# State-space decays by bfloat16 selector matmuls, in two decay and two score banks

## The reference, cut to what matters

```
a_cum = jnp.cumsum(dtc * A.reshape(SSM_GROUPS, SSM_HPG), axis=2)
diff = a_cum[:, :, :, None] - a_cum[:, :, None]
decay = jnp.exp(jnp.where(tril, diff, -jnp.inf))
cb = jnp.einsum('bclgn,bcsgn->bclsg', Cc, Bc)
y_diag = jnp.einsum('bclsgj,bcsgjp->bclgjp', cb[..., None] * decay, xdt)
```

## Time and profile before

| | |
|---|---|
| median of three runs | 2743.5 us |
| span of the profiled execution, first to last instruction | 2729.7 us |
| the median less that span (launch and end; the profile shows no more of its execution) | 13.8 us |
| conv, group a / group b | until about 114 us / 681 to 815 us |
| ssd, group a / group b | 114 to 170 us / 815 to 905 us |
| busy over the span: TensorE / VectorE / ScalarE / GpSimd | 74% / 53% / 25% / 54% |
| mean granted TensorE clock | 0.870 |

### The profile page before, as it was taken

How to read it: one execution, slowest core, us unless ns; L and a number is a source line. 1 busy time by engine, 2 the same in 40 slices (tenths; PEclk the granted TensorE clock), 3 DMA queues, 4 the chain that set the end, 5 groups by cost and what they waited for, 6 DMA issues and landing times. The chain is left out here.

```text
span 2729.7 us, 31629 instructions
## 1 busy us (share of the span) xinstructions
PE 2018.4 (74%) x10995; PEld 1286.9 (47%) x10995; DVE 1456.9 (53%) x3506; ACT 673.6 (25%) x2035; POOL 1478.6 (54%) x1493
## 2 busy tenths in 40 slices
PE   8999989987977979989988946755267776655044
PEld 6888875655655656654444722322144443111010
DVE  3331013226897975457731568778686665106910
ACT  4441016313547320015531112321011110001000
POOL 1120000006556766656654777787867777567775
PEclk9899989988988999989989967886588987868577
DMA  5414344344895899889889979999999999999998
GB/s 181 169 62 140 129 179 186 134 164 168 302 345 190 323 391 400 326 339 331 333 328 398 347 250 374 411 394 341 398 343 412 409 411 402 402 401 402 409 409 326
DMA packets 209780, 843.32 MB, mean 309 GB/s; under 512 B 25752, under 2 KB 32728, under 8 KB 190104
## 3 DMA queue, kind: packets, MB, share of 16 engines
q0 software_dynamic: 170912, 644.95, 61.8%
q1 hardware_dynamic: 38712, 196.36, 19.3%
HBM read 821.80 MB, written 23.54 MB: 310 GB/s over the span
## 5 line engine op out<-in xcount | busy, mean ns | idle before, releaser
L3604 POOL DMA_INDIRECT e_ring<-in_peer_u,e_idx x523 | 615.2, 1176 | 300.1 <-DVE e_dot L3768 142.7
L3768 DVE CUSTOM_DVE_ANT_0 e_ring<-e_ring,e_h 128x1024 f32<-128x1024 f32 x523 | 631.5, 1243 | 68.7 <-PEq L1159 22.0
L3604 POOL DMA_INDIRECT e_ring<-in_peer_v,e_idxT x487 | 510.7, 1049 | 258.5 <-issue 132.4
L3671 PE MATMUL ps<-e_ring,e_wz 128*32 128x512 f32 x1948 | 316.8, 698 | 261.9 <-DMA e_ring<-in_peer_v,e_idxT 152.9
L3671 PEld LDWEIGHTS ps<-e_ring,e_wz 128*32 128x32 f32 x1948 | 66.9, 119 | 416.7 <-issue 405.5
L363 PE MATMUL ps<-hT_ahead,wb 128*128 128x320 f32 x384 | 110.6, 443 | 0.9 <-DMA wb<-in_weights 0.9
L363 PEld LDWEIGHTS ps<-hT_ahead,wb 128*128 128x128 f32 x384 | 72.9, 195 | 30.1 <-issue 2.7
L1815 POOL CAST ra_atf<-ra_at 128x32 f32<-128x32 uint32 x8 | 1.7, 211 | 149.7 <-DVE ra_hit L1808 149.7
L3812 DVE TENSOR_TENSOR e_x<-e_x,ps 128x512 f32<-128x512 f32 x10 | 6.4, 684 | 141.8 <-PE ps L3671 141.8
L1183 POOL MEMSET inda<- 128x256 f32 x1 | 0.3, 311 | 147.7 <-POOLq L4071 147.7
L3671 PE MATMUL ps<-ring_pair,e_wz 128*32 128x512 f32 x152 | 63.2, 730 | 17.2 <-DMA e_ring<-in_peer_v,e_idxT 11.3
(11 more groups left out here) (778 smaller groups left out, 4610.4 us busy)
## 6 DMA issues: line engine op xcount, KB each, us to landing
wb<-in_weights SPq DMA_DIRECT2D x65, 1024.0 KB, 7.3
e_ring<-in_weights SPq DMA_DIRECT2D x36, 1024.0 KB, 4.9
wb<-in_late_weights SPq DMA_DIRECT2D x6, 2048.0 KB, 10.9
room<-in_late_weights SPq DMA_DIRECT2D x6, 2048.0 KB, 15.7
h<-in_weights SPq DMA_DIRECT2D x10, 1024.0 KB, 8.3
xs<-in_weights SPq DMA_DIRECT2D x9, 1024.0 KB, 7.9
e_ring<-in_peer_u,e_idx POOLq DMA_INDIRECT x523, 8.7
e_ring<-in_peer_v,e_idxT POOLq DMA_INDIRECT x487, 10.6
```

The lines of the kernel that those rows point to most:

```text
L3604: nc.gpsimd.indirect_dma_start(out=self.room(place), out_offset=None, in_=k.peer_u if kind == "u" else k.peer_v, in_offset=off).then_inc(s ...
L3671: last = nc.tensor.matmul(k.ps[32 * b:32 * b + 32, self.SUMS + i, :], self.wz[:, at:at + 32], self.room(self.v_at[n])[:, 512 * i:512 * i + ...
L3768: v.tensor_tensor_reduce(uu, uu, self.h[:, tile % 2, :], 1.0, 0.0, ALU.mult, ALU.add, self.dot[:, tile % 2, t:t + 1]).then_inc(self.dotted, 1)
```

## The change

The running sums, with heads on the partitions, are made once per chunk in conv, in PSUM bank 4, three times over (partitions 0 to 31, 32 to 63, 64 to 95). VectorE splits each into three bfloat16 pieces whose sum is the float32 value, one on each block of 32 partitions. A matmul with a matrix of ones and zeros as one operand (`head_rows`, 96x32) then picks a head and adds the three pieces. The row term a_cum[l] becomes four such matmuls, with the pieces as the moving operand and a broadcast column of the selector as the weight; the column term -a_cum[s] becomes one matmul with the pieces as the weight and the negative selector, broadcast to 4x128, moving. Nothing is left for the bias, and one activation covers four heads. Decays and scores have two banks each, and the orders of TensorE and VectorE change.

```diff
+            for rows_of, fill in ((k.head_rows, 1.0), (k.head_rows_neg, -1.0)):
+                own(gp.memset(rows_of[:], 0.0))
+                for piece in range(PIECES_F32):
+                    own(gp.affine_select(out=rows_of[:], in_=rows_of[:], compare_op=ALU.not_equal, fill=fill,
+                                         base=-HEADS * piece, pattern=[[-1, HEADS]], channel_multiplier=1))
...
+                for i, t in enumerate(g.prompt):
+                    for lo in range(0, SPLIT, HEADS):
+                        last = nc.tensor.matmul(k.ps[lo:lo + HEADS, 4, P * i:P * i + P], k.da[:, t, :], k.cum[:], start=True,
+                                                stop=True)
...
+            def split_sums():
+                sums = k.ps[0:SPLIT, 4, 0:NP]
+                parts = [slice(HEADS * i, HEADS * i + HEADS) for i in range(PIECES_F32)]
+                own(v.tensor_copy(k.cum_pieces[:], sums))
+                own(v.tensor_tensor(k.cum_rest[:], sums, k.cum_pieces[:], ALU.subtract))
+                own(v.tensor_copy(k.cum_middle[:], k.cum_rest[:]))
+                own(v.tensor_tensor(k.cum_rest[:], k.cum_rest[:], k.cum_middle[:], ALU.subtract))
+                v.tensor_copy(k.cum_pieces[parts[1]], k.cum_middle[parts[1]])
+                v.tensor_copy(k.cum_pieces[parts[2]], k.cum_rest[parts[2]]).then_inc(split, 1)
...
+                if f == 9:
+                    split_sums()
...
+        DECAY, SCORE = [1, ex.TURN], [0, ex.SUMS]
...
-                if q:
-                    pe.wait_ge(exped, q)
-                bank = k.ps[:, 1, :].rearrange("p (h l) -> p h l", h=4)
+                if q >= 2:
+                    pe.wait_ge(exped, q - 1)
+                bank = k.ps[:, DECAY[q % 2], :].rearrange("p (h l) -> p h l", h=4)
+                sums = k.cum_pieces[:, P * c:P * c + P]
+                h0 = gr * PER + 4 * i
                 mm(bank, k.identb[:], k.later[:].rearrange("p (a l) -> p a l", a=1).broadcast_to([P, 4, P]),
                    start=True, stop=False, skip_group_check=True)
+                mm(bank, sums, k.head_rows_neg[:, h0:h0 + 4].rearrange("p (h a) -> p h a", a=1).broadcast_to([SPLIT, 4, P]),
+                   start=False, stop=False, skip_group_check=True)
                 for j in range(4):
-                    hh = gr * PER + 4 * i + j
-                    last = mm(bank[:, j, :], k.da[:, t0 + c, hh:hh + 1].broadcast_to([P, P]), k.cum[:],
+                    last = mm(bank[:, j, :], k.head_rows[:, h0 + j:h0 + j + 1].broadcast_to([SPLIT, P]), sums,
                               start=False, stop=(j == 3), skip_group_check=True)
...
-                if u:
-                    pe.wait_ge(weighted, 2 * u)
+                if u >= 2:
+                    pe.wait_ge(weighted, 2 * u - 2)
...
             for u in range(U + 1):
                 if u < U:
                     decays(u, 0)
+                    decays(u, 1)
...
-                if u:
-                    within(u - 1)
                 if u < U:
                     score(u)
                     ex.pe(2 * u)
-                    decays(u, 1)
                 if u:
+                    within(u - 1)
                     from_state(u - 1)
                     to_state(u - 1)
...
-                for j in range(4):
-                    hh = gr * PER + 4 * i + j
-                    last = a.activation(MT[:, q % 4, j, :], k.ps[:, 1, j * P:j * P + P], ACT.Exp,
-                                        bias=k.nacum[:, t0 + c, hh:hh + 1])
-                last.then_inc(exped, 1)
+                a.activation(MT[:, q % 4], k.ps[:, DECAY[q % 2], :].rearrange("p (h l) -> p h l", h=4),
+                             ACT.Exp).then_inc(exped, 1)
...
                 if u < U:
                     weigh(u, 0)
-                if u:
-                    finish(u - 1)
-                if u < U:
                     ex.dve(2 * u)
                     weigh(u, 1)
                 if u:
+                    finish(u - 1)
                     carry(u - 1)
```

More of the change, by code:

```diff
@@ L50 @@
 PKEYS = 128
+PIECES_F32 = 3
+SPLIT = PIECES_F32 * HEADS
 EPS = 1e-6
@@ L314, in stage_conv @@
                                    for i in range(5))
-        stepped, steps_copied, raw, raw_copied, abs_done, exp_done, plus_one, ln_done, step_done, summed, negated = (
+        (stepped, steps_copied, raw, raw_copied, abs_done, exp_done, plus_one, ln_done, step_done, summed, negated,
+         split) = (
             sem(n) for n in ("stepped", "steps_copied", "raw", "raw_copied", "abs", "exp", "plus_one", "ln", "step",
-                             "summed", "negated"))
+                             "summed", "negated", "split"))
         steps_by_head = k.Bs[0:HEADS, 0:N]
@@ L334, in stage_conv @@
         k.conv_done = dict(tailed=(tailed, F), activated=(activated, F), gathered=(gathered, B_TILES),
-                           written=(written, 32) if g.sample else None)
+                           split=(split, 1), written=(written, 32) if g.sample else None)
         @block.sync
@@ L626, in by_channel, with scores_of @@
             return t.rearrange("p (h q) -> p h q", q=HP)
+        DECAY, SCORE = [1, ex.TURN], [0, ex.SUMS]
+        assert g.first or ex.done + ex.tokens <= min(ex.u_at[P - 1], ex.v_at[0])
+        def scores_of(u):
+            return k.ps[:, SCORE[u % 2], 0:P]
         @block.gpsimd
@@ L687, in score @@
                 tok = slice(P * c, P * c + P)
-                if u:
-                    pe.wait_ge(weighted, 2 * u)
-                mm(k.ps[:, 0, 0:P], k.BT[:, gr, tok], k.CT[:, gr, tok], start=True, stop=True).then_inc(scored, 1)
+                if u >= 2:
+                    pe.wait_ge(weighted, 2 * u - 2)
+                mm(scores_of(u), k.BT[:, gr, tok], k.CT[:, gr, tok], start=True, stop=True).then_inc(scored, 1)
             def within(u):
@@ L720, in _ @@
             pe.wait_ge(*conv["tailed"])
+            pe.wait_ge(*conv["split"])
             for u in range(U + 1):
@@ L804, in weigh @@
                 dve.wait_ge(scored, u + 1)
-                s = k.ps[:, 0, 0:P].rearrange("p (a l) -> p a l", a=1).broadcast_to([P, 4, P])
+                s = scores_of(u).rearrange("p (a l) -> p a l", a=1).broadcast_to([P, 4, P])
                 dve.wait_ge(exped, q + 1)
@@ L4085, in allocate @@
     k.identb, k.later, k.causal = sb("identb", [P, P], BF16), sb("later", [P, P], BF16), sb("causal", [P, P], BF16)
+    k.head_rows, k.head_rows_neg = sb("head_rows", [SPLIT, HEADS], BF16), sb("head_rows_neg", [SPLIT, HEADS], BF16)
     k.same, k.cum_s, k.later_s = sb("same", [NS, NS]), sb("cum_s", [NS, NS]), sb("later_s", [NS, NS], BF16)
@@ L4110, in allocate @@
     k.hTs = k.mTs
+    flat = k.mTs[:].rearrange("p f n -> p (f n)")
+    k.cum_pieces, k.cum_middle = (flat[0:SPLIT, P * i:P * i + P].bitcast(BF16) for i in range(2))
+    k.cum_rest = flat[0:SPLIT, 2 * P:4 * P]
     k.xs, k.zs, k.Bs = sb("xs", [P, D_INNER]), sb("zs", [P, D_INNER]), sb("Bs", [P, WINDOW + NS])
```

## The result

In the first set the changed kernel took 2698.98 to 2717.28 us, median 2707.45, against 2743.55 for the kernel before: a ratio of 0.9887, 95% interval 0.9853 to 0.9920. The forecast was 2727 (2716 to 2741). The direction was right, the size was not: 36 us in this set where 16.3 were forecast. Over all sets, 22 executions of four copies of the changed kernel have a mean of 2709.8 us and 90 of the kernel before 2738.2: 28.4 us less, give or take 3. Two executions far out of line, one of 5092 us of the kernel before and one of 10431 us of `after_gates_early` (experiment 2), are in no mean or ratio here.

A forecast was written before the change was run, and what follows sets the result against it. TensorE was taken to bound group a, VectorE group b's conv, and nothing to be full in group b's ssd. Terms -9.5 + 1.3 - 8.2 + 0.1 = -16.3 from 2743.5 gave 2727 us, range 2716 to 2741.

The forecast's parts named there:

- so I keep the clock at 0.50 until 131.5: Group a's ssd: TensorE idles before 118 as before, so half clock stays until 131.5, with 6.7 us of work done by then.
- I take 5: Group b's ssd: VectorE's idle time falls from 14.9 us to 5, giving -9.9 us.
- Base: Whole kernel: the summed changes were subtracted from the median of 2743.5 us, 13.8 above the profiled span of 2729.7.
- Scan a, prices: Group a's ssd: decays 0.66 us instead of 1.11, units 4.19 and 5.05 us; with the clock assumption, -9.5 us.
- Rival 1: Group a's ssd: the clock doesn't fall, so the 6.7 us lost come back, 2720.5 us; chance 0.14.
- Conv a: Group a's conv: six added float32 matmuls cost +1.3 us on full TensorE; the split is hidden in VectorE's idle time.
- Conv b: Group b's conv: VectorE is full, so the split costs +2.3 us (0 to 3); the matmuls are hidden.
- Scan b: Group b's ssd: VectorE becomes the bound; -9.9 us of idle time and 0.6 more for the later finish, -10.5.
- rival 2: Group b's ssd: VectorE keeps its 14.9 us idle, waiting for ScalarE's scaling, and the split is paid: 2737 us; chance 0.19.
- Rival 3: Both ssd stages: TensorE runs at half clock throughout, so the kernel gets slower, 2766 us; chance 0.04.
- Start: Program start: GpSimd's extra memsets and selections, about 2.3 us, finish just in time for TensorE: +0.1 us (0 to 0.8).
- Later stages: Behind ssd: each stage carries fixed tokens, so late stages full of transfers start earlier and don't take back the saving.

The follow-up runs named there:

- after_gates_early: Changed kernel with the sample's sixteen small gate loads issued by SyncE one stage earlier: 0.9906 of the kernel before.
- experiment 2: Sixteen small gate loads of the sample's compressed attention issued one stage earlier: on the kernel before 1.0009 of its time, on the changed kernel 0.9906.
- conv_only: Kernel before plus only the selectors, the six matmuls and the split, with the old scan making no use of them: 1.0006 of the kernel before.
- banks_only: Kernel before with two banks each and the new orders, keeping float32 decays and four biased exponentials, nothing added in conv: 0.9921 of the kernel before.
- split_only: Kernel before with the bfloat16 pieces, selectors and single exponential, but one bank each and the old orders: 0.9959 of the kernel before.
- after_pe_old: Changed kernel with TensorE's old order in the scan, within ahead of the next score and second decays: mean 2727.1 us against 2709.8 for the changed kernel.
- the mixed one: Changed kernel with float32 decays, biased exponentials and no conv additions in group b, plus idle matmuls in scan a: 0.9912 of the kernel before, mean 2712.0 us.

## Why the prediction was wrong in size

The mechanisms of both scans were those forecast; sizes were not. Two terms failed above all: the clock in scan a ("so I keep the clock at 0.50 until 131.5", 6.7 us charged, 3.3 or nothing measured), and VectorE in scan b ("I take 5" of idle time, 3.2 measured, and a busy time left as it was that fell by 2.5). The base was a third. 25.3 us are found by stage where the sum had 16.3; the steps in order:

- **Base.** The sum started from 2743.5, the median of three executions. The mean of 90 is 2738.2. Of the 36 us of the first set 5.3 are this, and 2.3 that its four executions of the changed kernel were short ones. Counted from 2738.2 the forecast would be 2722, still 12 too high.
- **Scan a, prices.** Right: 0.66 us for a decays, 4.24 and 5.1 for a unit. The forecast's scan a is 46.9 us (114.0 to 160.9), 40.2 without the 6.7 of the clock, and where the clock held it took 40.0. By the Trainium skill ("TensorE: Matmul & The Clock Gate", "Back-to-back issue gap") the four short matmuls would have taken 81 ns each; the trace has 0.22 us for four, 55 each, and the measurement decides.
- **Scan a, clock.** The step "so I keep the clock at 0.50 until 131.5" failed. The low stretch is 6.8 us long or absent, not 13. It cost 3.3 us or nothing where 6.7 were charged. Rival 1, the clock that doesn't fall, is what four of seven profiled executions of this scan show; its 0.14 was too little, and as a case of its own it was wrongly framed, since both happen in one kernel.
- **Conv a.** The six matmuls were taken at a float32 price of 0.22 us each, 1.35. They took 0.57 us, 45.99 to 46.56, as the row below and the next instruction's start give it. Their three copies go to three blocks of 32 columns of the array. The split cost nothing in a, as forecast.
- **Conv b.** +3.4 us where +2.3 was forecast. VectorE's busy time grew by the 2.3 (113.9 to 116.3 us), and the six operations are 2.4 us in the trace (727.16 to 729.56). The other 1.2 are idle time, 1.1 of it the convolution waiting for ScalarE (22.6 to 23.7 us); the forecast had no such term. That the two convs are right in sum (3.6 forecast, 3.5 measured) is luck.
- **Scan b.** This is the term that was mis-sized most. In the middle of the scan "I take 5" for VectorE's idle time was 3.2, and the busy time, which the forecast left as it was, fell from 62.1 to 59.6. Over the whole scan idle time went from 99.9 - 83.4 = 16.5 to 85.7 - 81.4 = 4.3 and busy time fell by 2.0, 14.2 in this pair and 15.1 on the mean, instead of 10.5. Some 1.2 of the 2.0 are the experts' reductions, shorter each by 36 ns (last section). That VectorE becomes the bound, with ScalarE's scaling hidden, was right, against rival 2. Rival 3 did not come: the clock in b did fall, from 0.80 to 0.77 in the middle of the scan, but with VectorE busy 59.6 of 62.8 us there is little that it can cost. The Trainium skill's rule behind this rival ("TensorE: Matmul & The Clock Gate", "A second HAM failure mode: psum-queue depth-cycling"), that short idle gaps in a cycle through PSUM banks make the clock swing, may describe b; no run here shows it to cost time.
- **Start.** +0.1 forecast. GpSimd's constants took 3 us more, not 2.3, and TensorE began at 8.9 to 9.1 us instead of 8.3 to 8.5, waiting for the last of them; conv a began within 0.3 us of where it did.
- **Later stages.** The sum had no term for them. Zgate a to query a came out 2.3 us longer on average, 0.4 to 3.8 in single executions. Two of the 2.3 are TensorE's clock again: in the stages merge and query its granted clock is lower, as the rows below show. It isn't the time saved that is given back, for `conv_only`, whose scan a is as long as before, has the same 32.3 us for merge and 84.8 for query.

Merge and query of group a before, then changed:

```profile
510.80:541.70 30.90, 29.33 (x129) 25.32 (x129) 6.77 (x16) 3.80 (x9) 0.00 (x0) 0.95 0.61 228
585.45:669.45 84.00, 66.97 (x344) 59.41 (x345) 57.23 (x251) 26.72 (x74) 40.64 (x82) 0.91 0.38 128
```
```profile
498.60:530.90 32.30, 30.76 (x128) 26.27 (x129) 6.77 (x16) 3.78 (x9) 0.00 (x0) 0.91 0.59 217
574.70:659.45 84.75, 67.72 (x345) 59.93 (x346) 57.19 (x251) 26.72 (x74) 40.60 (x82) 0.88 0.38 127
```

The row of the six matmuls in conv a (two records each), and of the wait at the start:

```profile
45.99 0.64 PE L417 MATMUL ps<-cum,da 128*32 128x128 f32 x12
```
```profile
9.10 1.12 PE L284 MATMUL ps<-ident,na_x 128*128 128x128 f32 x4 [9.10 <-POOL dt L195]
```

**What stays open.** The timed difference is 28.4 us, give or take 3, and the stages give 25.3; the three profiled executions of before were 7 us below their kernel's mean, the four changed ones 4 below theirs, and that is the difference. More telling, the kernels with one part of the change (`banks_only`, `split_only`, `after_pe_old`) and the mixed one need some 7 to 12 us more behind the start of zgate b than the changed kernel does, in their profiled executions as by their means, though the code there is the same. In the profiles 4 to 6 of these us are the compressed attention of experiment 2, whose length proved to be worth nothing there. The experts' gathers and the other transfers fill the DMA engines there; no run isolates what differs.

## What to carry to other kernels

When two queues pass one buffer back and forth, ask which engine bounds the stage before counting cheaper instructions. In the stage bound by VectorE the second buffers and the order behind them gave 13 of 15 us, and the fourfold cheaper matmuls less than their preparation cost; in the stage bound by TensorE the cheaper matmuls gave most. Compare such stages at the same granted clock. Where an engine's clock falls after a wait, forecast both lengths of the stretch, and not the one that a single profile shows. Where the DMA engines were full, a wait removed from an engine was worth nothing, for the bytes were as many as before. And start a forecast from the mean of many executions.

## What the hardware showed that was not expected

- Six float32 matmuls of 128 columns into blocks of 32 columns of the array took 0.57 us together, against 0.22 each for those of the full array. Three ran side by side: their single records start in threes, 6 or 7 ns apart.
- The same code, with the same 2 us of idle time of TensorE, showed a stretch of 6.8 us at 1.2 GHz in three executions and none in four. The four began the scan some 0.3 to 1.5 us later.
- GpSimd's product of the carried state took 1445 ns in scan b before and 1044 ns after. In the same scan VectorE's reduction of an expert's rows took 1342 and 1306 ns. With VectorE's old order GpSimd's product is back at 1408 ns, and VectorE waits 2.7 us for it; with the banks and new orders alone it is 1040, with the split alone 1323. So it goes with VectorE's order. Before and after:

```profile
L653 POOL TENSOR_TENSOR h<-h,cdec 128x512 f32<-128x512 f32 x8 | 11.6, 1445 | 5.3 <-PE ps L710 5.3
```
```profile
L684 POOL TENSOR_TENSOR h<-h,cdec 128x512 f32<-128x512 f32 x8 | 8.3, 1044 | 4.8 <-PE ps L744 4.8
```

- Of sixteen small loads that SyncE issues at 0.3 us each, the fifteenth took 5.8 to 11.6 us in ten of sixteen profiled executions, those in which GpSimd had issued its large gather before it. With the loads a stage earlier the seventh took 8.0 us without such a gather, so what it stands behind was not isolated.
